# A two-layer decoder step: the mixer's projections in another order, decode samples and gating branch moved under them

## What is computed

```python
h = rmsnorm(x, W['mix_pre_g'][l]) * (1 + sc1) + sh1
z, xbc, dt_raw, u, v, ga, gb = split_cols(h @ W['w_in'][l], IN_SIZES)
ya, hs, cs = ssd_branch(z, xbc, dt_raw, conv0[l], ssm0[l], ...)
yb, vr = chunk_mlp_branch(jax.nn.gelu(u), jax.nn.gelu(v), W['cmlp_ln_g'][l], ...)
merged = jax.nn.sigmoid(ga) * (ya @ W['w_ssd_out'][l]) + jax.nn.sigmoid(gb) * (yb @ W['w_cmlp_out'][l])
x = x + g1 * rmsnorm(merged @ W['w_o'][l], W['mix_post_g'][l])
```

## Time and profile before

| what | value |
|---|---|
| median of 3 runs (1924.02 to 1928.8) | 1926.07 us |
| profiled execution: time, span | 1930.64 us, 1928.3 us |
| mean granted clock of the profiled execution | 0.944 |
| busy: PE, DVE, ACT, POOL | 1761.1, 1336.6, 1028.2, 68.1 us |
| layer 0: first projection matmul to first of ssd_out | 48.7 to 352.4 us |
| layer 1: the same | 691.0 to 966.1 us |
| mixture of experts, from 1070 to 1902 us: PE busy | 821.44 of 832.00 us |

### The profile page before, as it was taken

How to read it: one execution, slowest core, us unless ns; L and a number is a source line. 1 busy time by engine, 2 the same in 40 slices (tenths; PEclk the granted TensorE clock), 3 DMA queues, 4 the chain that set the end, 5 groups by cost and what they waited for, 6 DMA issues and landing times.

```text
span 1928.3 us, 33789 instructions
## 1 busy us (share of the span) xinstructions
PE 1761.1 (91%) x13192; PEld 1634.2 (85%) x13192; DVE 1336.6 (69%) x1658; ACT 1028.2 (53%) x1045; POOL 68.1 (4%) x108
## 2 busy tenths in 40 slices
PE   6999979769999879997786999999999999999995
PEld 4888978658989869987685899989898989899993
DVE  3355767754445456786756688878887888788884
ACT  2344734333333335473342676767676776777771
POOL 4000110000000000020000000000000000000000
PEclk8999988889999979998886899999999999999997
DMA  9897652347886526573240999999999999999980
GB/s 282 259 279 239 204 165 66 120 129 221 282 284 207 163 67 196 165 223 128 66 137 28 311 351 348 357 294 351 347 348 313 337 347 348 334 319 353 344 308 23
DMA packets 379497, 465.06 MB, mean 241 GB/s; under 512 B 10403, under 2 KB 351603, under 8 KB 379378
## 3 DMA queue, kind: packets, MB, share of 16 engines
q1 hardware_dynamic: 372370, 441.65, 70.1%
q0 software_dynamic: 6720, 20.86, 3.5%
q10 hardware_dynamic: 304, 1.08, 0.2%
HBM read 452.84 MB, written 10.92 MB: 240 GB/s over the span
## 4 chain that ended last, share of the span: by engine, by line
PE 79%; DVE 11%; ACT 4%; DMA 4%; issue 2%; POOL 0%; SPq 0%; ACTq 0%; DVEq 0%; POOLq 0%
PE psum L403 9%; PE psum L1143 9%; PE psum L1148 9%; PE psum L1145 9%; PE psum L414 9%; PE psum L408 8%; PE psum L1167 4%; PE psum L1171 4%; PE psum L1168 4%; PE psum L746 2%; PE psum L443 2%; DMA ce<-in_state_ssm_dram 1%; PE psum L1102 1%; DVE ce L1755 1%; DMA out_ssm_s_dram<-ce 1%
## 5 line engine op out<-in xcount | busy, mean ns | idle before, releaser
L369 DVE TENSOR_TENSOR wlo<-raw,whi 128x2048 fp32r<-128x2048 f32 x219 | 501.6, 2291 | 107.9 <-ACT whi L364 107.0
L364 ACT ACTIVATE whi<-raw 128x2048 fp32r<-128x2048 f32 x219 | 418.4, 1912 | 31.6 <-PE psum L1171 30.0
L347 DVE TENSOR_TENSOR wlo<-raw,whi 128x2048 fp32r<-128x2048 f32 x113 | 258.9, 2291 | 247.2 <-ACT whi L342 246.7
L403 PE MATMUL psum<-xhi,whi 128*128 128x264 f32 x1584 | 232.6, 301 | 39.5 <-ACT xhi L1231 37.1
L342 ACT ACTIVATE whi<-raw 128x2048 fp32r<-128x2048 f32 x113 | 216.9, 1919 | 89.8 <-PE psum L414 64.5
L403 PEld LDWEIGHTS psum<-xhi,whi 128*128 128x128 f32 x1584 | 211.8, 198 | 62.0 <-issue 48.1
L408 PE MATMUL psum<-xlo,whi 128*128 128x264 f32 x1584 | 214.3, 289 | 0.0
L414 PE MATMUL psum<-xhi,wlo 128*128 128x264 f32 x1584 | 211.1, 286 | 0.0
L408 PEld LDWEIGHTS psum<-xlo,whi 128*128 128x128 f32 x1584 | 205.5, 195 | 0.0
L1143 PE MATMUL psum<-whi,hghi 128*128 128x256 f32 x1408 | 202.4, 286 | 3.2 <-issue 2.3
L414 PEld LDWEIGHTS psum<-xhi,wlo 128*128 128x128 f32 x1584 | 197.9, 188 | 0.1
(11 more groups left out here) (354 smaller groups left out, 1911.8 us busy)
## 6 DMA issues: line engine op xcount, KB each, us to landing
raw<-in_exp_wd_dram SPq DMA_DIRECT2D x76, 1024.0 KB, 5.1
raw<-in_exp_wg_dram SPq DMA_DIRECT2D x72, 1024.0 KB, 6.7
raw<-in_exp_wu_dram SPq DMA_DIRECT2D x72, 1024.0 KB, 6.9
raw<-in_w_in_dram SPq DMA_DIRECT2D x52, 1024.0 KB, 5.3
raw<-in_w_mod_dram SPq DMA_DIRECT2D x17, 1024.0 KB, 5.5
hf<-in_exp_wu_dram SPq DMA_DIRECT2D x16, 1024.0 KB, 6.5
hf<-in_exp_wg_dram SPq DMA_DIRECT2D x16, 1024.0 KB, 6.7
hf<-in_exp_wd_dram SPq DMA_DIRECT2D x12, 1024.0 KB, 4.9
```

The costliest lines, as they stand in the source:

```text
L347: dve.tensor_tensor(wlo[slot], raw[slot], whi[slot].bitcast(F32), ALU.subtract) \
L364: act.activation(whi[j % R3], raw6[slot], ACT.Copy).then_inc(sem["hi_ready"], 1)
L369: dve.tensor_tensor(wlo[j % R3], raw6[slot], whi[j % R3].bitcast(F32), ALU.subtract) \
L403: pe.matmul(out, whi[slot][:, k, j * P:(j + 1) * P], hi(k), start=first and k == 0, stop=False)
```

## The change

The change does not touch what is computed. It writes the mixer's order anew on every engine:

- Projections in the order dt, xbc, z, v, u, ga, gb. Softplus and the convolution (now in nine pieces) run under xbc and z.
- The samples run from z's last chunk to ga's second. ACT now scales the state in place (`scale`, eight ACTIVATE with a scale of their own) beside `outer`; DVE adds the two (one instruction of 128x1024), multiplies with C (two of 128x512) and sums (one reduce). B and C rows share one PSUM bank.
- Three state buffers, the halves of ce and hT. POOL issues fetches 2, 0 and 1 first, and each later fetch b+2 behind store b-1.
- v's mean and variance are taken under u; its gain and bias move from DVE to ACT (eight Identity in ga's first `after`). The transposes, spatial products and the gating of u run under ga and gb, the first chunk's token turn behind gb's second chunk, its decays' spread behind the third, its exponentials on ACT ahead of gb's last epilogue. w_spatial is turned under z into a buffer of its own.
- y and state of chunk 0 stand between cmlp_out's first and second chunk, those of chunk 1 between the third and the fourth; the fourth stands ahead of the gate norm's sums on PE, and DVE takes it out behind them. The second chunk's tokens are turned inside the second cmlp_out chunk.
- The product of ce with C moves from DVE to POOL, and the exponential of ce is split in halves.
- The router's weights load with the first parameters; the first w_mod buffer moves from xdw to sgb.

The core of the diff:

```diff
-        for name in ("xbc", "dt", "v", "u", "z", "ga", "gb"):
+        for name in ("dt", "xbc", "z", "v", "u", "ga", "gb"):
...
-        sring = ce[:, :, :].rearrange("p (s k) n -> p s k n", s=2)
+        sring = [ce[:, 0:KT, :], ce[:, KT:2 * KT, :], hT[:, :].rearrange("p (k n) -> p k n", k=KT)]
...
                 for b in range(B):
-                    s = b % 2
-                    if b >= 2:
-                        pool.wait_ge(s_out[s], 16 * (l * B // 2 + b // 2))
-                        pool.wait_ge(sem["samp_used"], l * B + b - 1)
-                    pool.dma_start(sring[:, s], state[b]).then_inc(s_in[s], 16)
...
+                    pool.wait_ge(sem["s_new"], l * B + b + 1)
+                    pool.dma_start(new[b], sring[b % SR3]).then_inc(s_out[b % SR3], 16)
+                    if 1 <= b < B - 2:
+
+                        pool.wait_ge(s_out[(b - 1) % SR3], 16 * (l * PER[(b - 1) % SR3] + (b - 1) // SR3 + 1))
+                        pool.wait_ge(sem["samp_used"], l * B + b)
+                        fetch_state(b + 2)
...
+                for g in (1, 0):
+                    pool.wait_ge(sem["ce_exp"], 2 * (l + 1) - g)
+                    ins = pool.tensor_tensor(ce[:, g * R:(g + 1) * R, :], ce[:, g * R:(g + 1) * R, :],
+                                             bc(xcv[:, KT + G + g, Q:2 * Q], 1, [P, R, Q]), ALU.mult)
+                ins.then_inc(sem["ce_ready"], 1)
...
+                cmlp_chunk(0)
+                y_and_state(0)
+                cmlp_chunk(1, next_tokens)
+                spread_cum(1)
+                cmlp_chunk(2)
+                y_and_state(1)
+                cmlp_chunk(3)
...
+                def scale(b):
+
+                    act.wait_ge(s_in[b % SR3], 16 * (l * PER[b % SR3] + b // SR3 + 1))
+                    for k in range(KT):
+                        ins = act.activation(sring[b % SR3][:, k, :], sring[b % SR3][:, k, :], ACT.Copy,
+                                             scale=spx[:, k, b:b + 1])
+                    ins.then_inc(sem["outer_ready"], 1)
...
+                def after_v(c):
                     outer(c + 1)
+                    scale(c + 1)
+
+                def after_u(c):
+                    if c == 1:
+                        act.wait_ge(sem["v_centered"], l + 1)
+                        act.activation(hf[:, :, :], vb[:, :, :], ACT.Square).then_inc(sem["v_sq"], 1)
+                        outer(5)
+                        scale(5)
+                    if c == 2:
+                        scale(6)
+                    if c == 3:
+                        scale(7)
...
+                    dve.wait_ge(sem["outer_ready"], OUT[b] + 2 * l * B)
+                    dve.tensor_tensor(Sb, Sb, sprod[s], ALU.add).then_inc(sem["s_new"], 1)
+                    dve.wait_ge(sem["s_new"], l * B + b + 1)
+                    for g in range(G):
+                        ks = slice(g * KT // G, (g + 1) * KT // G)
+                        ins = dve.tensor_tensor(sprod[s][:, ks, :], Sb[:, ks, :], bc(Cb[:, g, :], 1, [P, KT // G, NS]), ALU.mult)
+                    then(ins)
+                    dve.tensor_reduce(ysm[:, :, b], sprod[s], AX.X, ALU.add).then_inc(sem["samp_used"], 1)
```

More of the change, by code:

```diff
@@ L471, in mod_keep, with act_phase @@
                 .then_inc(sem["mod_added"], 1)
-        def act_phase(act, key, count, epilogue=None, peel=0, end=False, after=None):
+        def act_phase(act, key, count, epilogue=None, peel=0, end=False, after=None, ahead=None):
             n0, q0 = N0[key], Q0[key]
@@ L920, in _, with spatial @@
-                pe.wait_ge(sem["w_ready"], l + 1)
-                pe.matmul(ms[:, 0, 0:2 * KT], ones[0:KT, :], diag[:, :, :].rearrange("g a b -> g (a b)"), start=True,
-                          stop=True).then_inc(sem["sp_bcast"], 1)
-                pe.wait_ge(sem["sp_bcast_ready"], l + 1)
-                for c in range(NQ):
+                def spatial(c, b0):
                     for k in range(KT):
-                        out = ms[:, 2 * c + k // 4, (k % 4) * Q:(k % 4 + 1) * Q]
+                        out = ms[:, b0 + k // 4, (k % 4) * Q:(k % 4 + 1) * Q]
@@ new lines, in after_ga @@
+                def after_ga(c):
+                    if c == 0:
+                        act.wait_ge(sem["v_root"], l + 1)
+                        for t in range(KT):
+                            ins = act.activation(vb[:, t, :], vb[:, t, :], ACT.Identity, bias=row("cmlp_ln_b", l, t),
+                                                 scale=row("cmlp_ln_g", l, t))
+                        ins.then_inc(sem["v_normed"], 1)
+                    if c < 2:
+                        outer(6 + c)
+                    if c == 1 or c == 2:
+                        act.wait_ge(sem["v_tok"], l * NQ + c)
+                        act.activation(vtok[:, c - 1, :], msf[:, 1024:2048], ACT.Copy).then_inc(sem["v_tok_ready"], 1)
+                    if c == 3:
+                        act.wait_ge(sem["vs_turned"], l + 1)
+                        act.activation(vrow, msf[0:B, 1024:2048], ACT.Copy).then_inc(sem["vs_copied"], 1)
@@ new lines, in decays, with after_gb, ahead_gb @@
+                    act.activation(mix[:, 0:R, :], mix[:, 0:R, :], ACT.Exp).then_inc(sem["mix_exp"], 1)
+                def after_gb(c):
+                    if c == 2:
+                        keep_b(0)
+                def ahead_gb(c):
+                    if c == 3:
+                        decays(0)
+                        act.wait_ge(sem["sp_taken"], l + 1)
+                        act.wait_ge(sem["w_used"], N0["cmlp_out", l])
+                        hi_of_x(5 * l + 2, ub)
+                gates("z", zs, ACT.Silu, after_z)
@@ L1701, in after_v, with conv @@
                         dve.tensor_copy(spin[:, 2 * B:2 * B + 1], headp[:, 2, l:l + 1]).then_inc(sem["cum_ready"], 1)
-                def conv(tiles, done=False):
+                def conv(*tiles):
+                    q = Q0["xbc", l] + tiles[-1] // MT
+                    dve.wait_ge(acc_free[q % 2], q // 2 + 1)
                     for k in range(CK):
```

589 lines of the change are left out of this document (312 added, 277 removed).

## The result

The changed kernel takes 1946.14 us (1940.86 to 1946.98, 4 runs) against 1927.43 us of the kernel before in the same comparison: ratio 1.0089, 95% interval 1.0072 to 1.0106. By the ratio it is slower by about 17 us (the medians lie 18.7 apart), above the forecast range of 1899 to 1934. The profiled execution took 1946.77 us with a span of 1944.9.

A forecast was written before the change was run, and what follows sets the result against it. TensorE was taken as the bound, with idle time and a lowered clock as losses. Changes of -13.6 (layer 1), -3.5 (layer 0) and +6 us (clock) sum to -11.1, from median 1926.07 to 1915 us; range 1899 to 1934.

The forecast's parts named there:

- six fold waits: Layer 0, v and u: folds wait for ScalarE's modulation copy; 2.8 each in v1 to v3, v0 4.3, u0 4.1, u2 3.4 us.
- The scale: ScalarE's eight 128x128 ACTIVATEs scaling a state in v and u: taken at 2.1 us, bounds 1.6 and 2.7.
- ga1: Second ga chunk, layer 1: waits 6.2 us for a split queued behind the last state's scale; layer 0 1.5 us.
- ga2: Third ga chunk: waits 3.6 us for its split, behind v's gain and bias and outer 6 on ScalarE.
- norm chain: Tail, ahead of ssd_out: the chain stays and TensorE waits 5.2 us, against 3.63 before for its first half alone.
- the stretch behind gb: Sign of being right: from gb's end to cmlp's first matmul falls from 27 us to under 4.
- half-rate matmuls through v and u: Sign of being wrong: TensorE's matmuls run at half clock through the v and u projections.
- the terms of v1 and u0: Layer 1 chunk stalls from ScalarE's load: v1 2.9 us with Silu and table load, u0 2.1 us with table load.
- Clock after the new stalls: Both layers: half-rate TensorE time behind new waits, mostly filled by later waits; 3 us a layer, bounds 0 and 8.
- No change: Rival: each of 12 new stalls costs 2.7 us at half rate, half filled; 16 us instead of 6, 1925; chance 0.20.
- More is gained: Rival: scale at 1.6 us saves 8 us, no half rate after stalls under 3 us saves 6; 1901; chance 0.20.
- Slower, by the transfers: Rival: weights, modulation chunks and states exceed DMA bandwidth in v and u; 14 and 9 us more, 1938; chance 0.15.

The follow-up runs named there:

- experiment 10: Changed kernel with state scaling, ce's products and v's gain and bias on VectorE, modulation copy and keeping ahead of the splits: 1883.21 us, 0.9784 of the kernel before.
- Experiment 3: Changed kernel with dummy matmuls added on TensorE ahead of five fold waits in layer 0: 1940.72 us.
- experiment 2: Changed kernel with the state scaled on VectorE instead of ScalarE, three buffers and all orders kept: 1909.29 us, 0.9908 of the kernel before.
- experiment 5: Changed kernel with the modulation copy ahead of outer and scale on ScalarE, and the keeping ahead of the low split on VectorE: 1919.55 us.
- experiment 6: Changed kernel with states scaled on VectorE, and both modulation copy and keeping moved ahead of the splits: 1901.69 us.
- experiment 1: Changed kernel with layer 0's modulation copy moved ahead of outer and scale on ScalarE: 1939.95 us.
- experiment 4: Changed kernel with ce's two products moved from GpSimd to VectorE, each just ahead of mix's product: 1943.27 us.

## Why the prediction was wrong

**Where the time was to go: right.** Layer 0's idle time was forecast at 37.4 us and measured at 36.7, layer 1's at 29.0 and 27.4. The six fold waits were priced at 4.3 + 8.4 + 4.1 + 3.4 = 20.2 and came to 19.8, each within 0.5 us of its own term. The scale was dearer than taken (2.47 against 2.1); in layer 1 ga1 (4.49 against 6.2) and ga2 (2.83 against 3.6) more than gave that back. In the tail y waited 3.24 us (3.0) and the norm chain 1.41 + 3.62 (5.2). Of the signs that were named, the stretch behind gb, the folds and the gate norm came as written, and ga1 fell short of its 5 to 7 us; one sign of being wrong came too, the half-rate matmuls through v and u. Two readings were off without weight in the sum: the terms of v1 and u0 add up to 2.8 and 2.2 (2.9 and 2.1 stood there), and the rows of B and C take as many matmuls after as before, 64 in the two layers (L873, now L869).

**The step that failed: "Clock after the new stalls", with "I take 3 us a layer; bounds 0 and 8".** The sum took all half-rate time of the kernel before out, 16 and 12 us, and put 3 back in each layer. TensorE's work at the high clock was estimated well: weighting the busy time of windows of 5 us by their granted clock gives some 262 us in layer 0 and 233 in layer 1 of either kernel (an estimate; 262.8 and 232.5 were taken). So the half-rate time after the change is 287.2 - 262 = 25 us and 246.7 - 233 = 14 us, where 3 and 3 stood. That is 33 us more than was put in; less 2.3 us of idle time under the forecast and 2.6 us outside the mixers it is about 28. The span came out 16.6 us longer where 11.1 shorter was forecast, 27.7 apart.

Two things were wrong in it. First, the half-rate time does not all leave with the waits that were removed. In experiment 10, with 10.3 and 13.0 us of idle left, TensorE is still busy 269.6 and 240.0 us, some 7 us a layer over its work: the waits that stay (y, ssd_out, the one ahead of the layer) keep theirs, and some of it follows no wait at all. PE's timeline in layer 0's tail of the changed kernel:

```profile
336.42 3.83 PE L912 MATMUL psum<-dth,ident 16*128 16x128 f32 x32
340.18 2.96 PE L404 MATMUL psum<-xhi,whi 128*128 128x264 f32 x16
342.94 2.93 PE L409 MATMUL psum<-xlo,whi 128*128 128x264 f32 x16
```

The spread of the decays is 32 narrow matmuls (16 of 128 partitions) that run 3.8 us without a pause at a granted clock of 1.00; then, still without idle time, the clock is granted at 0.71 and 0.67, and groups that take 2.1 us in full-speed rows take 2.96 and 2.93. In experiment 10 the group behind the same spread takes 3.61 us at 0.54.

Second, new waits do not fill each other. The text held that a wait behind half-rate work is "mostly filled"; here each chunk's wait is set by ScalarE's queue, which starts anew at the end of every chunk (its epilogue waits 4.83 us for L415 in the rows above), so slow matmuls in one chunk only move the next wait on. Experiment 3 prices it: 16.3 us of waits cost 8.4 us behind them.

**The rivals.** The mechanism of "No change" (each new stall costs half-rate time) was the true one; its price, 16 us in place of 6, was too small because it counted from the same base: 39 us were measured. "More is gained" failed on both of its conditions, a scale of 1.6 us and no half rate behind short stalls. "Slower, by the transfers" was on the right side for a reason that did not occur: in v and u of layer 0 no engine waited for a raw tile or, there, for a state, and the DMA share was under the 0.78 of before (0.67 over the two). The last state's fetch did show in layer 1, as ScalarE's wait of 2.95 us for state 7, inside ga1's 4.49.

**What the change is worth.** Without the scale on ScalarE, it makes the kernel faster by 0.9% (experiment 2). What the moved gating branch and the cover of the gate norm are worth by themselves no run separates; the rows show the stretches of 28.8 and 27.0 us behind gb at 1.5 and the wait of 3.87 us gone. What made it slower is 2.47 us of work put into the one queue behind which the copy, the split and so TensorE stand. Moving two short instructions ahead in two queues recovers 27 us (experiment 5), moving the scale back to VectorE 37 (experiment 2). The two do not simply add (44 together, experiment 6), since both remove the same waits. With ce's products and the gain on VectorE as well it is 63 us in all (experiment 10).

Not settled: which idle time brings the clock down and which does not, and why the waits of experiment 1 cost half as much as those of the changed kernel. Waits of 1.4 us left it alone, and one of 2.35 us in layer 1 (the group behind it, at 790.00, takes 2.21); of two waits of 2.79 us alike in length, one was followed by a group of 2.73 and one by 3.87.

## What to carry to other kernels

Price a change by the queue that it lengthens, not by the engine's busy share: ScalarE was busy 53% of the span before the change, and 2.5 us more per chunk, ahead of a copy that TensorE wanted, cost 37 us. When a wait is cured by moving an instruction forward, look for the same lateness in the next queue before counting the gain (experiment 1 moved 18.5 of 19.8 us). And carry the half clock as a cost of each new wait, between a third of it again (experiment 1) and nearly as much (experiment 10) in these runs, besides what stays behind narrow matmuls when no wait is left.

## What the runs showed of the hardware

A product on GpSimd holds VectorE up. In the tail above, GpSimd multiplies from 953.89 for 2.38 us, and a split that takes 2.28 us elsewhere, begun at 955.01, takes 3.40: it ends 2.14 us after GpSimd was done. From 957.97 GpSimd multiplies for 2.69 us, and two products of 1.22 us on VectorE take 4.53, ending 2.21 us after GpSimd. With GpSimd's products gone, the split takes 2.27 and a product 1.21 (experiment 4). The Trainium skill ("SBUF — State Buffer", on the shared port pair) says that the two engines share a port pair that is held for a whole instruction, where VectorE reads two inputs from SBUF against a GpSimd operation that reads it. These rows agree. The prediction had not weighed it.

Eight scalings of 128x128 in SBUF take 2.47 us on ScalarE where eight of the same shape out of PSUM take 2.18, and eight of 128x264 with a gain and a bias per partition take 4.1 us, where VectorE's eight of 128x264 took 2.7 in the kernel before.

TensorE's clock is granted lower not only behind idle time: behind 3.8 us of narrow matmuls without a pause it was 0.71 and 0.67 in the changed kernel and 0.54 in experiment 10.
